# A two-layer diffusion backbone on one core: separate sum buffers, residuals eight tokens late, all query units ahead, three exponential buffers

## The reference

```
q      = u @ wq                          # 8 heads, two halves of 128
s1, s2 = q halves against 128 keys each  # top 16 of each
top_s, pos = top_k(v1[i] + v2[j], 16)    # 16 of the pairs, a number in 0..16383 each
g      = softmax(top_s)
h      = gelu(eu[expert] . u)            # 8 heads x 16 experts = 128 rows of eu
y      = sum over 128 experts of g * h * ev[expert]
```

## Time and profile before

| | |
|---|---|
| median of 3 runs | 3305.12 us (3304.79 to 3307.26) |
| profiled execution | 3309.81 us, of which the span is 3308.0 us |
| PE / DVE / ACT / POOL busy | 77% / 58% / 15% / 29% of the span |
| granted TensorE clock, mean | 0.769 of full |
| DMA | 1023.54 MB, mean 309 GB/s |
| chain that ended last | PE 43%, DVE 22%, DMA 21%, POOL 7%, issue 5% |
| L2059 (dot products, DVE) | 1536 of 685 ns |
| L1207 (broadcasts, PE) | 1536 of 483 ns |
| L1189 (weighing, PE) | 3072 of 918 ns |

### The profile page before, as it was taken

One profiled execution on the slowest core, in us unless ns is written; L12 is line 12 of the kernel. 1 busy time (PEld: TensorE's weight loads), 2 busy tenths in 40 slices (PEclk: granted clock), 3 DMA queues, 4 the chain that ended last, 5 costly groups with the idle time before them and its releaser, 6 DMA issues.

```text
span 3308.0 us, 34175 instructions
## 1 busy us (share of the span) xinstructions
PE 2532.0 (77%) x11632; PEld 1311.7 (40%) x11632; DVE 1906.8 (58%) x6120; ACT 493.9 (15%) x1065; POOL 970.9 (29%) x968
## 2 busy tenths in 40 slices
PE   7879985687899979758889877776897667666556
PEld 5758883153455535214445421112687211111011
DVE  3648988745444466785444455554338765555555
ACT  2141121113222111002022210001412000000000
POOL 0820001267222222222943223331000233333332
PEclk7989997696799979658889965656998665665665
DMA  7606734896799989786999989998140699989997
GB/s 303 236 30 264 300 159 188 335 394 245 295 391 384 385 326 370 284 323 251 344 374 402 420 341 398 401 404 346 44 136 20 262 357 399 405 350 405 391 404 310
DMA packets 147887, 1023.54 MB, mean 309 GB/s; under 512 B 18816, under 2 KB 19328, under 8 KB 28032
## 3 DMA queue, kind: packets, MB, share of 16 engines
q0 software_dynamic: 110592, 805.36, 61.5%
q1 hardware_dynamic: 30496, 202.36, 15.6%
q10 hardware_dynamic: 6624, 13.64, 1.1%
HBM read 1011.32 MB, written 9.96 MB: 309 GB/s over the span
## 4 chain that ended last, share of the span: by engine, by line
PE 43%; DVE 22%; DMA 21%; POOL 7%; issue 5%; ACT 2%; SPq 0%; ACTq 0%; DVEq 0%; POOLq 0%
DMA ring<-in_peer_uv,eT 20%; PE PS L1189 11%; PE PS L875 7%; DVE ring L2059 6%; PE PS L1207 5%; POOL ring L714 5%; PE PS L810 3%; PE PS L1082 2%; PE PS L1035 2%; PE PS L880 2%; PE PS L896 2%; PE PS L1124 1%; PE PS L948 1%; DVE ring L1616 1%; POOL mix L598 1%
## 5 line engine op out<-in xcount | busy, mean ns | idle before, releaser
L2059 DVE CUSTOM_DVE_ANT_0 ring<-ring,PS 128x512 f32<-128x512 f32 x1536 | 994.0, 685 | 867.9 <-PE PS L1207 506.4
L714 POOL DMA_INDIRECT ring<-in_peer_uv,eT x768 | 729.8, 950 | 2204.8 <-PE PS L1189 1345.8
L1207 PE MATMUL PS<-xr,onesb 3*128 3x512 bf16 x1536 | 641.2, 483 | 434.7 <-DVE hcol L2059 393.8
L1189 PE MATMUL PS<-ring,zcol 128*32 128x512 f32 x3072 | 596.7, 918 | 102.7 <-DVE zcol L2069 100.0
L1207 PEld LDWEIGHTS PS<-xr,onesb 3*128 3x128 bf16 x1536 | 114.5, 96 | 1042.2 <-DVE hcol L2059 584.6
L1189 PEld LDWEIGHTS PS<-ring,zcol 128*32 128x32 f32 x3072 | 104.5, 144 | 407.2 <-issue 228.1
L875 PE MATMUL PS<-uT,W 128*128 128x256 f32 x1024 | 254.3, 398 | 8.0 <-issue 8.0
L1549 ACT ACTIVATE ge<-hdot 128x4 f32<-128x4 f32 x192 | 39.4, 205 | 1397.7 <-DVE hdot L2064 1397.5
L875 PEld LDWEIGHTS PS<-uT,W 128*128 128x128 f32 x1024 | 196.2, 197 | 66.2 <-issue 36.3
L1616 DVE CUSTOM_DVE_ANT_0 ring<-ring 128x1024 f32<-128x1024 f32 x160 | 205.7, 1326 | 8.3 <-DMA ring<-in_w_rows 3.5
L810 PE MATMUL PS<-uT,W 128*128 128x256 f32 x672 | 166.3, 401 | 17.1 <-ACT uT L1271 17.1
(11 more groups left out here) (239 smaller groups left out, 2398.3 us busy)
## 6 DMA issues: line engine op xcount, KB each, us to landing
ring<-in_w_rows SPq DMA_DIRECT2D x40, 1024.0 KB, 8.0
W<-in_w_in SPq DMA_DIRECT2D x30, 1024.0 KB, 9.2
W<-in_w_gate SPq DMA_DIRECT2D x16, 1408.0 KB, 8.2
W<-in_w_gate SPq DMA_DIRECT2D x16, 1280.0 KB, 7.6
ring<-in_w_q SPq DMA_DIRECT2D x16, 1024.0 KB, 12.6
W<-in_w_gate SPq DMA_DIRECT2D x16, 1024.0 KB, 10.2
W<-in_w_out SPq DMA_DIRECT2D x12, 1024.0 KB, 5.1
ring<-in_peer_uv,eT POOLq DMA_INDIRECT x768, 9.4
```

The source lines that it names most:

```text
L714: pool.indirect_dma_start(ring[:, slot, :], None, (peer_uv0, peer_uv1)[b.l], bass.IndirectOffsetOnAxis(eT[:, f % 2, t:t + 1], 0)).then_inc ...
L1189: last = T.matmul(PS[k * NR:(k + 1) * NR, (6 + h) * 512:(7 + h) * 512], zcol[:, g % 2, k, NR - 1 - at:2 * NR - 1 - at], ring[:, slot, D + ...
L1207: T.matmul(bank(x_bank(q, n) + h), onesb[32 * k:32 * k + 3, :], xr[32 * k:32 * k + 3, g % 2, h * 512:(h + 1) * 512], start=True, stop=True)\
L2059: V.tensor_tensor_reduce(out=u_half, in0=u_half, in1=bank(x_bank(q, n) + h), scale=1.0, scalar=0.0, op0=ALU.mult, op1=ALU.add, accum_out=h ...
```

## The change

Five things change. (1) A tile's sums have their own buffer, `ysb` for tile one and `nvf_c` (the context's value projections, not read at that time) for tile two; both are copied in the expert stream, and `limit` grows by 128 after every residual. (2) `after` takes a slack: residuals of LAT0 (both), CTX0 (first) and LAT1 (first) come eight tokens after the tile. (3) All 16 query units of tile two stand ahead of "tile ready". (4) The share of a `late` step is 2.4 instead of 1.2. (5) Attention has three exponential buffers, `transposed` and `values` are one job later, the loop has one more step, and for the context `scores(n+1)` comes last in a step.

```diff
+SLACK = 2 * GRP
 SCRIPT = [...
-          ("after", 0, 0), ("residual", LAT0, 0), ("after", 0, 1), ("residual", LAT0, 1),
+          ("after", 0, 0, SLACK), ("residual", LAT0, 0), ("after", 0, 1, SLACK), ("residual", LAT0, 1),
...
-          ("after", 1, 0), ("residual", CTX0, 0), ("after", 1, 1), ("residual", CTX0, 1),
+          ("after", 1, 0, SLACK), ("residual", CTX0, 0), ("after", 1, 1, 0), ("residual", CTX0, 1),
...
-          ("after", 2, 0), ("residual", LAT1, 0), ("after", 2, 1), ("residual", LAT1, 1)]
+          ("after", 2, 0, SLACK), ("residual", LAT1, 0), ("after", 2, 1, 0), ("residual", LAT1, 1)]
-         "late": 1.2}
+         "late": 2.4}
-                while self.done < turn * TOK + (tile + 1) * P:
+                while self.done < turn * TOK + (tile + 1) * P + slack:
-            if what == "residual" and args[1]:
-                self.limit += TOK
+            if what == "residual":
+                self.limit += P
+        y_of = [ysb[:, :], nvf_c[:, :, :].rearrange("p t n -> p (t n)")]
+        def exp_of(s, n):
+            if s:
+                return part(scr, n % 3 * 2 * TOK, [2, TOK])
+            return part(scr, n % 3 * D, [2, 2 * TOK]) if n % 3 < 2 else part(ysb, 0, [2, 2 * TOK])
 # TensorE and ScalarE, apart
-                for u in range(AHEAD):
+                for u in range(16):
                     unit(1, u)
...
+                scores(1, 3)
...
                 yield TILE_READY
                 for q in range(LATE):
-                    u = AHEAD + q
-                    if u < 16:
-                        unit(1, u)
-                    if u == 13:
-                        scores(1, 2)
-                    if u == 16:
-                        scores(1, 3)
                     yield "late"
 # TensorE, back
-                for n in range(len(JOBS) + 2):
-                    if n + 1 < len(JOBS):
+                for n in range(len(JOBS) + 3):
+                    if s == 0 and n + 1 < len(JOBS):
                         scores(n + 1)
-                    if 1 <= n <= len(JOBS):
-                        transposed(n - 1)
-                    if n >= 2:
-                        values(n - 2)
+                    if 2 <= n < len(JOBS) + 2:
+                        transposed(n - 2)
+                    if n >= 3:
+                        values(n - 3)
+                    if s == 1 and n + 1 < len(JOBS):
+                        scores(n + 1)
                     yield "job"
 # ScalarE: probs(n - 2) and outputs(n - 3) in place of n - 1 and n - 2; residual and experts:
-                if tt:
-                    act.wait_ge(weighed, (ORDER.index(f) + 1) * NG)
-                    act.wait_ge(a["x_new"], a.at("x_new", 1))
-                    A(ysb[:, :], two(6), ACT.Copy).then_inc(y_out, 1)
...
-                            if g == NR - 1:
-                                act.wait_ge(weighed, q * NG + NR)
+                            if g % NR == NR - 1:
+                                tt = g // NR
+                                act.wait_ge(weighed, q * NG + g + 1)
                                 if q:
                                     r = at_of["residual", ORDER[q - 1]]
-                                    act.wait_ge(r["x_new"], r.at("x_new", TT))
-                                A(ysb[:, :], two(6), ACT.Copy).then_inc(y_out, 1)
+                                    act.wait_ge(r["x_new"], r.at("x_new", tt + 1))
+                                A(y_of[tt], two(6), ACT.Copy).then_inc(y_out, 1)
 # VectorE: bounded(n) fills exp_of(s, n) and waits for the transposes of job n - 3
-                    if n >= 2:
-                        dve.wait_ge(a["ptp"], a.at("ptp", n - 1))
+                    if n >= 3:
+                        dve.wait_ge(a["ptp"], a.at("ptp", n - 2))
 # normed(n): the scaled identities keep two buffers
                     dve.wait_ge(a["exp"], a.at("exp", n + 1))
+                    if n >= 2:
+                        dve.wait_ge(a["ptp"], a.at("ptp", n - 1))
 # VectorE residual: y_of[tt] in place of ysb throughout
```

More of the change, by code:

```diff
@@ L125, in __init__ @@
     def __init__(self):
-        self.seen, self.ready, self.done, self.limit = [], 0, 0, TOK
+        self.seen, self.ready, self.done, self.limit = [], 0, 0, TT * P
     def token(self, experts):
@@ L135, in run @@
             if what == "after":
-                turn, tile = args
-                while self.done < turn * TOK + (tile + 1) * P:
+                turn, tile, slack = args
+                while self.done < turn * TOK + (tile + 1) * P + slack:
+                    assert self.done < min(self.ready, self.limit)
                     self.token(experts)
@@ L291, in build @@
         t5 = part(scr, 0, [5, TOK])
-        Sm = part(scr, 0, [2, 2, 2 * TOK])
         PT = part(mix, 14 * TOK, [4 * TOK])
         gbuf = part(scr, 0, [2, NB, TOK])
+        y_of = [ysb[:, :], nvf_c[:, :, :].rearrange("p t n -> p (t n)")]
         mT = part(mix, 18 * TOK, [KD, TOK])
@@ L431, in row_banks, with s_of @@
             return (4, 4, 4) if f == LAT1 and tt == 0 else (2, 4, 2)
-        def s_bank(s, n):
-            return 6 if s == 0 and n % 2 else 2
+        def s_of(s, n, e):
+            return bank((6 if s == 0 and n % 2 else 2) + e)
+        def exp_of(s, n):
+            if s:
+                return part(scr, n % 3 * 2 * TOK, [2, TOK])
+            return part(scr, n % 3 * D, [2, 2 * TOK]) if n % 3 < 2 else part(ysb, 0, [2, 2 * TOK])
         def x_bank(q, n):
@@ L1023, in scores @@
                         for e in range(2):
-                            last = T.matmul(bank(at + e, m * TOK, (m + 1) * TOK), of_q[rows_[e], c, qt * P:(qt + 1) * P],
+                            last = T.matmul(s_of(s, n, e)[:, m * TOK:(m + 1) * TOK], of_q[rows_[e], c, qt * P:(qt + 1) * P],
                                             k_[rows_[e], :], start=True, stop=True)
@@ L1456, in back @@
                 act.wait_ge(pch_s, gated[b.front])
-                for n in range(len(JOBS) + 2):
+                for n in range(len(JOBS) + 3):
                     if n < len(JOBS):
                         exps(n)
-                    if 1 <= n <= len(JOBS):
-                        probs(n - 1)
-                    if n >= 2:
-                        outputs(n - 2)
+                    if 2 <= n < len(JOBS) + 2:
+                        probs(n - 2)
+                    if n >= 3:
+                        outputs(n - 3)
                     yield "job"
@@ L1801, in normed @@
                     for e in range(2):
-                        last = V.tensor_scalar(stage_c[:, q, e * P:(e + 1) * P], ident[:, :], st[:, q, 10 + e:11 + e], None,
+                        last = V.tensor_scalar(stage_c[:, d, e * P:(e + 1) * P], ident[:, :], st[:, q, 10 + e:11 + e], None,
                                                ALU.mult)
```

33 lines of the change are left out of this document (15 added, 18 removed).

## The result

The changed kernel takes 3256.98 us (median of 4 runs, 3256.35 to 3265.08) beside 3306.19 us of the kernel before on the same chip: ratio 0.9853, 95% interval 0.9836 to 0.9869, so 49 us or 1.5% faster. Forecast were 3245 us and a range of 3208 to 3288. The profiled execution took 3256.35 us (span 3254.5; before 3308.0), so the two traces, which differ by 53.5 us, show all of the gain and some 4 us more than the medians do.

A forecast was written before the change was run, and what follows sets the result against it. Transfers were taken to set the 2.6 us per tail token, with DMA room elsewhere. Terms 12 + 9 + 10 + 9 + 10 + 10 = 60 us took 3309.8 to 3250; with the median 4.7 lower, 3245 was predicted, range 3208 to 3288.

The forecast's parts named there:

- Attention of LAT0 and LAT1: Unwoven latent attention: transpose spacing falls from 5.30 to 4.4 us, gaining 6 us in each, 12 together.
- the deduction of up to 3.1 for a later start: Latent attention: first transposes start later by at most 3.1 us, cutting the 9.9 us gain to 6.8.
- The prediction's lower bound: Latent attention: the first jobs may gain nothing because of the low clock, 0 us each.
- Attention of the context: Woven context attention: TensorE's new order shortens 15 steps to 6.5 us each, gaining 9 us, between 0 and 27.
- near 97: Expected sign in the context's attention: the stage takes near 97 us instead of 107.
- Late steps of LAT1: LAT1: tile two ready 15 us later with 10 more tokens, 26 us less tail; gain 10, between 0 and 20.
- Late steps of LAT0: LAT0: tile two ready 15 us later, 24 us back in the context's selection; gain 9, between -5 and 15.
- Rival E: Late steps: late tokens keep costing 5.0 us each, so the kernel is 9 us slower, 3314; chance 0.08.
- Residuals of LAT0: LAT0's residuals: 31 us for 14 tokens worth 37 of tail, plus 4 for the ring; gain 10, between -5 and 21.
- First residuals: First residuals of CTX0 and LAT1: slack removes VectorE's 6.22 us wait; 5 us each, 10 together, between 0 and 18.
- D: Residuals: slack doesn't do what it says, because the residual's body is what costs; 20 us less, 3265; chance 0.14.
- rival C: Whole kernel: more gain in context attention, residuals and late steps, 95 us in all, 3210; chance 0.14.

The follow-up runs named there:

- att_only: The kernel before with the attention edit alone (third exponential buffer, transposes and values one job later, context's scores last): 3271.99 us, ratio 0.9901.
- old_lag: The changed kernel with its three exponential buffers, but transposes and values back at one and two steps, scores first: 3262.44 us, ratio 0.9859.
- late_only: The kernel before with all sixteen query units of tile two ahead and the late share 2.4, nothing else: 3302.55 us, ratio 0.9987.
- units_only: The kernel before with all query units of tile two ahead of tile ready, late share still 1.2: 3296.55 us, ratio 0.9956.
- late12: The changed kernel with the late share back at 1.2, all query units still ahead: 3237.8 us, ratio 0.978.
- late22: The changed kernel with a late share of 2.2 instead of 2.4: 3232.38 us, ratio 0.9777.
- sums_only: The kernel before with a buffer for each tile's sums, the limit growing by 128 and the slack of eight tokens: 3288.5 us, ratio 0.9945.
- slack0: The changed kernel with the slack set to 0, buffers and limit kept: 3268.33 us, ratio 0.9883.

## Why the prediction came out

The direction and the size held, 49 us measured for the 60 forecast. Of the single terms only the context's attention came within 2 us of its forecast: the latent attention and CTX0's residual brought more, the late steps and LAT0's residuals less, and these errors largely cancelled. That the sum is so near is in part luck. In the order of its steps, each stage read between the same events of both traces:

**Attention of LAT0 and LAT1: 12 forecast, 25 measured (mis-sized).** 76.8 to 62.7 us and 71.6 to 60.5, from the first score product to the last output copy. The spacing came as forecast, 4.38 for 4.4, and 11 spacings by 0.92 are 10.1 in each. What failed was the deduction of up to 3.1 for a later start: it isn't seen. In LAT1 the gain is the spacings and 1 us. LAT0 gained 3 more, and these lie in its first two spacings, 7.45 and 7.46 us before and 4.48 and 4.39 after, where TensorE had a granted clock of 0.62 in the first 23 us before and 0.75 in the first 22 after. Its first two transposes before:

```profile
175.83 3.42 PE L1035 MATMUL PS<-stage_c,scratch 128*128 128x128 f32 x16 [1.80 <-DVE stage_c L1802]
...
183.28 3.78 PE L1035 MATMUL PS<-stage_c,scratch 128*128 128x128 f32 x16 [2.97 <-DVE stage_c L1802]
```

The second takes 3.78 us where it takes 2.02 after. The prediction's lower bound let the first jobs gain nothing, for the low clock; they gained the most.

**Attention of the context: 9 forecast, 11 measured.** 118.0 to 107.0 us, with 28 tokens for 27. The prediction had the stage at 107 before, since its window (745 to 852) began 10 us behind the first score product, so the sign "near 97" did not come though the gain did. The two attention terms are 36 together, and `att_only` measured 33 by itself. The reason given, the order of TensorE's work, holds: VectorE's waits for a broadcast, up to 4.22 us, are fewer and 3.72 us at most (the prediction had 2), and `old_lag` shows that the buffer by itself brings nothing here. But in the changed kernel the order brings 4.5 of the 11 us, and the other 6 came with the late edits (118.0 to 111.8 in `late_only`). Traces with the old attention and the old share differ by 3 us here (118.0 in the kernel before, 114.7 in `units_only`), so these parts are rough.

**Late steps of LAT1: 10 forecast.** Tile two is ready 15.5 us later with nine tokens more in the stage, as forecast (15). But the stage was forecast from the kernel before, which charged the units' 7 us to the tokens: it was 7 for the units and 23 for the tokens, not 0 and 15, and that the difference fits is luck. From tile one ready to the end of the span LAT1 takes 735.7 us before, 724.4 in `late12`, 718.1 in `late22` and 728.4 in the changed kernel. So late edits and slack together gained 7.3 of the 15 forecast. The units bring 7 of the 11.3 in `late12`. Eight tokens more at the good position bring 6.3; ten at the bad one lose 4. Ten tokens cost 22.8 us, 2.3 each, and save 2.62 each: 3.4 in all, and the pause and what follows from it take more than that. The 2.3 is a mean of 1.8 for the first eight and 4.3 for the last two.

**Late steps of LAT0: 9 forecast, nothing measured.** 15.9 us paid, and 31 tokens' front of 101.9 us became 33 tokens' of 116.1: 14 us that I had at nothing (6 to 14 in the six traces with this share). From there to the context's tile two ready 20 us came back (forecast 24). From tile one of LAT0 to tile two of the context ready the gain is 951.1 - 940.3 = 10.8 us, and the 11 of the context's attention lie in that stretch; the late term itself is 0. Rival E, by which late tokens would go on costing 5.0 us, didn't hold for the 2.3 of the mean: units, not transfers, were what the gathers waited for. It comes near for the last two.

**Residuals of LAT0: 10 forecast, about 2 measured.** From tile two of the context ready to the second residual's end, 22.1 us became 48.4 for 12 tokens; from the same start up to the end of the latent's convolutions, where the first residual of CTX0 is due, 35.1 us more hold 14 tokens, whose tail would be 36.7. The prediction had 31 us for the 14 tokens and 4 back for a ring less dry; but the woven stage behind the residuals got 8.8 us longer (399.9 to 408.7) for two tokens more in it, so nothing came back. The x rows still end an idle time of 6.48 us, and GpSimd's pause is 43.31 us where it was 51.99. Timeline of the changed kernel:

```profile
1468.43 1.01 PE L1213 MATMUL PS<-xr,onesb 3*128 3x512 bf16 x2 [6.48 <-DMA xr<-xrows]
...
1479.63 0.94 POOL L725 DMA_INDIRECT ring<-in_peer_uv,eT  x1 [43.31 <-PE PS L1195]
```

**First residuals: 5 for CTX0, 9 measured; 5 for LAT1, at most 4.** In CTX0, 384.8 us for 142 tokens became 339.4 for 128: 45.4 less, of which 36.7 are the 14 tokens. In LAT1, 613.2 us for 229 tokens became 589.9 for 220: 23.3 less, of which 23.6 are the nine tokens. That is nothing for the slack, with the longer pause in it; in `late12`, without that pause, 11.3 less the units' 7 leave 4, and `sums_only` shows 4 too. VectorE's wait of 6.22 us is gone as forecast. What is left is the body, 17.9 us from its first operation to its last where it was 17.1, with a wait of 4.01 us before the last (3.75 before the change):

```profile
2914.24 1.22 DVE L2031 TENSOR_TENSOR ysb<-ysb,PS 128x1024 f32<-128x1024 f32 x1
...
2930.87 1.22 DVE L2044 TENSOR_TENSOR X<-ysb,PS 128x1024 f32<-128x1024 f32 x1 [4.01 <-PE PS L792]
...
2937.05 0.94 POOL L725 DMA_INDIRECT ring<-in_peer_uv,eT  x1 [13.70 <-PE PS L1195]
```

The body still holds GpSimd for 13.70 us (16.67 before). This is what D said of this place, and D has its half: `slack0` puts the slack at 10 us of the forecast 20 for all residuals. How 6.22 us of a wait came to be 4 us or less of the stage is not shown.

The measured terms are 25 + 11 + 0 + 2 + 9, and 7 for LAT1 from tile one on: 54 in all, against 60 forecast and 53.5 between the spans. The attention's surplus of 15 us and CTX0's of 4 stand against 25 by which the late steps and the residuals of LAT0 and LAT1 fell short. One slip of the prediction's sums has no effect: the terms of rival C add up to 96 and not 95.

On transfers, the prediction weighed a limit of about 358 GB/s per core (the Trainium skill, DMA: Bandwidth & Descriptors, Where 436 GB/s comes from) against the 397 of the earlier trace rows. The section gives that figure as a half of what two cores share, and the page's own measurements with the other core idle go up to 425, so the page is less at odds with this trace than the prediction said; what the other core did is in no run here. The changed kernel shows 392 over 303 us and 390 over 322: the measurement decides again, and a tail token costs 2.6 us, not the 2.9 estimated from the 358.

## What to carry to other kernels

Find the last item that still pays and stop there: two tokens fewer in each late stage gave 25 us here, half as much as the whole change, since the last two cost 4.4 us each where the eight before them cost 1.8. Where a ring is freed in groups, look also at the position in the group at which a stage hands over; it is worth 4.5 us of pause each time here, and how much more is open. Price each half of a combined edit by itself; "units ahead" (+14.6) and "more tokens late" (about -24 in the changed kernel) looked like one gain of 19. Before moving work out of a tail, divide what it costs in front by its tail price: at 2.3 against 2.6 there is almost nothing to be had, and even at 1.8 against 2.6 `late22` is not faster than `late12` beyond error. And do not read a whole kernel's gain from one stage: what the slack won at LAT0's residuals, the next stage took back.

## What the hardware showed that I had not expected

The gathers nearly keep their pace next to far more compute than in a tail: 363 GB/s in the late stage of `late22` with VectorE's selection and TensorE's units beside them, against 390 to 397 in the tails.

The granted clock of TensorE is near its lower level (1.2 GHz; the upper is 2.4) where the kernel waits for transfers, 0.59 in the tails and 0.54 in the late steps, and 0.85 to 0.89, mostly the upper level, in the woven stages of the context's front and of the latent's next one; the clock of the whole execution was 0.773 after, 0.772 in `late12` and 0.769 in `late22`. So the clock of the whole does not follow the time: it is highest in the slowest of the three. In a single stage it can matter, as in the context's front, where TensorE is busy for nine tenths of the time and the same code took 108.0 us at 0.90 and 116.1 at 0.85.
